# Two transformer blocks on one core: the second tile's norm as a sum of two scaled terms, and four reorderings

## The reference, cut to what matters

```python
def rms_norm(x, g):
    y = x * rsqrt(mean(x * x) + EPS)
    return y * g

h = rms_norm(x, g[0]); m = mixer(h)
x = x + rms_norm(m, g[1])           # post norm, residual
h = rms_norm(x, g[2])               # pre norm of the feed-forward layer
x = x + rms_norm(squared_relu_mlp(h, w1, w2), g[3])

def squared_relu_mlp(h, w1, w2):
    return square(relu(h @ w1)) @ w2
def conformer_conv(h, ...):         # second mixer: three biases are added
    u = h @ w_pw1 + b_pw1           # gate, 31-tap convolution + b_dw, layer norm, silu
    return u @ w_pw2 + b_pw2
```

## Time and profile before

| | |
|---|---|
| median of 3 runs | 923.44 us (922.0 to 924.53) |
| profiled execution, its time | 923.78 us |
| its span | 922.0 us |
| TensorE matmuls busy | 901.8 us, 98% |
| VectorE busy | 689.9 us, 75% |
| POOL, ACT busy | 284.0 us, 268.9 us |
| HBM | 173 GB/s over the span |
| mean granted TensorE clock | 0.997 |

### The profile page before, as it was taken

The page is one execution under the profiler, slowest core; times in us unless marked ns, Lnnn a source line. Parts: engine busy times, 40 slices in busy tenths (PEclk is TensorE's granted clock), DMA queues, the critical chain, the costliest instruction groups (busy, mean ns, idle before and its releaser), DMA issues.

```text
span 922.0 us, 13057 instructions
## 1 busy us (share of the span) xinstructions
PE 901.8 (98%) x4934; PEld 756.7 (82%) x4934; DVE 689.9 (75%) x725; ACT 268.9 (29%) x550; POOL 284.0 (31%) x182
## 2 busy tenths in 40 slices
PE   8999999999999999999999999999999999999997
PEld 6987788888887787688888888888867888888886
DVE  5779879777777775769877777669787687676774
ACT  3537441111112511342111111455586411111112
POOL 5100055444442332136444443200000243333331
PEclk9999999999999999999999999999999999999999
DMA  8851625655558265216655555366502356556641
GB/s 290 283 204 79 219 85 200 226 182 182 182 195 276 99 208 183 92 46 228 201 200 198 200 200 178 107 226 215 219 1 81 104 196 216 190 179 211 192 137 46
DMA packets 82376, 160.29 MB, mean 174 GB/s; under 512 B 5065, under 2 KB 40667, under 8 KB 82337
## 3 DMA queue, kind: packets, MB, share of 16 engines
q1 hardware_dynamic: 82176, 159.68, 50.5%
q10 hardware_dynamic: 160, 0.07, 0.0%
HBM read 158.68 MB, written 1.05 MB: 173 GB/s over the span
## 4 chain that ended last, share of the span: by engine, by line
PE 85%; DVE 8%; ACT 3%; issue 2%; POOL 1%; DMA 1%; DVEq 0%; SPq 0%; POOLq 0%; ACTq 0%
PE ps L1930 82%; PE ps L1934 3%; DVE w_lo L750 2%; ACT arena L1480 1%; DMA x_res<-in_x 1%; ACT w_hi L1476 1%; POOL st L638 0%; ACT arena L1831 0%; DVE nrm L839 0%; DVE st L1292 0%; DVE act_hl L1101 0%; DVE x_res L836 0%; ACT arena L1627 0%; POOL st L637 0%; DVE arena L1416 0%
## 5 line engine op out<-in xcount | busy, mean ns | idle before, releaser
L750 DVE TENSOR_TENSOR w_lo<-raw,w_hi 128x2048 fp32r<-128x2048 f32 (+3 forms) x140 | 325.9, 2354 | 40.0 <-POOL w_hi L731 21.7
L1930 PE MATMUL ps<-act_hl,w_hi 128*128 128x512 f32 (+1 forms) x1088 | 242.0, 369 | 3.6 <-DVE act_hl L909 2.6
L1930 PEld LDWEIGHTS ps<-act_hl,w_hi 128*128 128x128 f32 x1088 | 183.7, 191 | 33.8 <-issue 3.6
L1930 PE MATMUL ps<-w_hi,hl 128*128 128x512 f32 (+2 forms) x680 | 186.7, 384 | 0.6 <-DVE w_lo L750 0.6
L617 POOL TENSOR_SCALAR w_hi<-raw 128x2048 fp32r<-128x2048 f32 x56 | 137.3, 2452 | 157.3 <-PE ps L1930 148.5
L1930 PE MATMUL ps<-w_hi,act_hl 128*128 128x512 f32 (+3 forms) x656 | 181.1, 381 | 2.4 <-DVE w_lo L750 2.4
L1930 PEld LDWEIGHTS ps<-w_hi,hl 128*128 128x128 f32 (+1 forms) x680 | 125.7, 189 | 24.0 <-issue 0.8
L1930 PEld LDWEIGHTS ps<-act_hl,w_lo 128*128 128x128 f32 x1024 | 135.9, 190 | 8.4 <-DVE w_lo L750 0.3
L1930 PEld LDWEIGHTS ps<-w_hi,act_hl 128*128 128x128 f32 x656 | 118.6, 188 | 27.0 <-issue 4.1
L1930 PE MATMUL ps<-act_hl,w_lo 128*128 128x256 f32 (+1 forms) x1024 | 139.4, 281 | 0.0
L1930 PE MATMUL ps<-w_lo,hl 128*128 128x512 f32 (+1 forms) x356 | 108.4, 378 | 0.0
(11 more groups left out here) (212 smaller groups left out, 741.0 us busy)
## 6 DMA issues: line engine op xcount, KB each, us to landing
raw<-in_mlp_w SPq DMA_DIRECT2D x64, 1024.0 KB, 5.2
raw<-in_w_gate SPq DMA_DIRECT2D x22, 512.0 KB, 3.9
raw<-in_w_up SPq DMA_DIRECT2D x22, 512.0 KB, 4.9
raw<-in_w_down SPq DMA_DIRECT2D x11, 1024.0 KB, 5.0
raw<-in_odd_w_pw SPq DMA_DIRECT2D x16, 512.0 KB, 5.4
raw<-in_w_in SPq DMA_DIRECT2D x8, 1024.0 KB, 6.1
raw<-in_even_w_in SPq DMA_DIRECT2D x6, 1024.0 KB, 5.6
raw<-in_even_w_out SPq DMA_DIRECT2D x4, 1024.0 KB, 6.8
```

The source lines that it names most:

```text
L750: tt(w_lo[slot_of(n)][:, 0:w], raw[slot_of(n)][:, 0:w], w_hi[slot_of(n)][:, 0:w].bitcast(F32), ALU.subtract).then_inc(S("w_split"), 1)
L1930: return pe.matmul(o, l, r, start=start, stop=stop, skip_group_check=True)
```

## The change

Seven edits; none changes what is computed beyond rounding.

1. **Second tile at boundaries 1 and 3.** Instead of `x = x + g*r; n = x*p` (g the gained output, r the post scale, p the pre gain), the tile's norm is `n = (g*p)*r + x*p`. `x*p` goes to a scratch tile `pre_1` in one 128x1024 operation behind the first tile's norm; `g` goes to a scratch tile `post_1`; `g*p` is made by halves before r is known; then two operations give `n`, and two more add the residual afterwards.
2. **Opening, ACT and VectorE.** ACT squares tile 0's half, then writes tile 0's high parts, and only then squares both halves of tile 1; VectorE no longer squares tile 1.
3. **Opening, POOL.** The copy of piece 1 goes ahead of rsqrt 1.
4. **First MLP's end.** The last piece is split before `bias_low(0)`.
5. **Second mixer.** The four bias matmuls move into `turn_normed`, ahead of the transpose of tile 1's fifth group.
6. **Third mixer's entry.** The low parts of pieces n and n+1 for tile 1 follow their high parts at once, and free their buffers there.
7. **Third mixer's entry.** Piece n+4's product takes the terms of `w_lo` last, and waits for the split only before them.

```diff
                 def first_rsqrt(m):
-                    gp.wait_ge(S("first_sq"), m + 1)
-                    gp.wait_ge(S("second_sq"), m + 1)
+                    gp.wait_ge(S("first_sq"), 2 * m + 1)
+                    gp.wait_ge(S("second_sq"), 1)
...
                 first_rsqrt(0)
-                hi_until(0)
+                hi_until(1)
                 first_rsqrt(1)
...
+                def gain_half_1(h):
+                    g = norms[0]
+                    dve.wait_ge(S("ssq"), ssqs[0] + h + 1)
+                    link(tt(post_1[:, half[h]], tall_out(ACC, 1)[:, half[h]], gain[g % 4][:, half[h]], ALU.mult))
+                def pre_half_1(h):
+                    link(tt(nrm[:, 1, half[h]], post_1[:, half[h]], gain[(norms[0] + 1) % 4][:, half[h]], ALU.mult))
+                def add_pre_1(g):
+                    next_rstd()
+                    ssqs[0] += 4
+                    for h in half:
+                        stt(nrm[:, 1, h], nrm[:, 1, h], rs_post[:, 1:2], pre_1[:, h], ALU.mult, ALU.add)\
+                            .then_inc(S("normed"), 1)
+                    for h in half:
+                        stt(x[:, 1, h], post_1[:, h], rs_post[:, 1:2], x[:, 1, h], ALU.mult, ALU.add)\
+                            .then_inc(S("x_new"), 1)
...
                     if s in SCALE_LATER:
                         post_add_pre(s, 0, g + 1)
+                        link(tt(pre_1, x[:, 1, :], gain[(g + 1) % 4][:, :], ALU.mult))
+                        gain_half_1(0)
                     else:
                         post_add(0)
                         pre_tile(0, g + 1)
-                    post_gain(1, 0)
+                        post_gain(1, 0)
                     low_tile(0, TURN_BANK[s])
-                    post_gain(1, 1)
                     if s in SCALE_LATER:
-                        post_add_pre(s, 1, g + 1)
+                        pre_half_1(0)
+                        gain_half_1(1)
+                        pre_half_1(1)
+                        add_pre_1(g + 1)
                     else:
+                        post_gain(1, 1)
...
                 first_norm(0)
-                first_square(1)
                 first_low(0)
...
+                    lo_until(n0 + 4 * MLP_BLOCKS - 1)
                     if s == 0:
-                        lo_until(n0 + 4 * MLP_BLOCKS - 2)
                         bias_low(0, bias_pw1)
-                    lo_until(n0 + 4 * MLP_BLOCKS - 1)
...
+                act.wait_ge(S("x_in0"), 16)
+                first_square(0, 0)
+                act.wait_ge(S("gain_col"), 1)
+                first_high(0)
+                act.wait_ge(S("x_in1"), 16)
+                first_square(1, 0)
+                first_square(1, 1)
+                first_high(1)
...
+                            if m == 1 and k == 4:
+                                for b in range(4):
+                                    mm(ps[:, ACC + b, :], sel[:, b % 2, :], bias_pw2, True, False)
...
                         narrow(j, m, False)
+                        if m == 1 and j < 2:
+                            narrow(j, 1, True).then_inc(S("pe_piece"), 1)
                 lows[0] += TILE_LOWS
-                for j in range(4):
-                    if j >= 2:
-                        arrived(n + j)
-                        narrow(j, 0, True)
+                for j in range(2, 4):
+                    arrived(n + j)
+                    narrow(j, 0, True)
                     narrow(j, 1, True).then_inc(S("pe_piece"), 1)
...
-                    tall(n + 4 + q, UP, act_hl, 2 * q, q == 0, q == 3, 2, 1024)
+                    tall(n + 4 + q, UP, act_hl, 2 * q, q == 0, q == 3, 2, 1024, low_last=q == 0)
```

More of the change, by code:

```diff
@@ L302, in two_blocks @@
         gain_rows = AR(2048, P, p=KD)
+        post_1, pre_1 = AR(4608, D), AR(5632, D)
         gain_col = st[:, 176:176 + KD]
@@ L1536, in high_of_turned, with first_square, first_high @@
                         act_high(turned(bank, 2 * j, 2), 2 * j, 2)
[L1539 to L1544, removed]
+                def first_square(m, h):
+                    f(junk[:, m, 512 * h:512 * h + 512], x[:, m, 512 * h:512 * h + 512], ACT.Square, scale=1.0 / D ** 0.5,
+                      accum_out=ssx[:, 2 * m + h:2 * m + h + 1]).then_inc(S("first_sq"), 1)
+                def first_high(m):
                     for k0 in range(0, KD, TILE_STEP[m]):
@@ L2378, in _ @@
                 turn_normed()
-                for m in range(M):
-                    for h in range(2):
-                        mm(ps[:, ACC + 2 * m + h, :], sel[:, h, :], bias_pw2, True, False)
                 tall(FIRST["pw2"], ACC, act_hl, 0, False, False, 2, 1024, k_waits=(lows[0] + 1, lows[0] + 2))
```

## The result

The changed kernel takes 926.72 us (median of 6 runs, 926.22 to 927.63) against 923.43 us before (median of 6, 922.0 to 924.53): a ratio of 1.0042, 95% interval [1.0031, 1.0052]. It is slower by 0.42%, just beyond the 0.3% that was called no change. The time is 0.9 us over the forecast of 925.8 and inside its range, but it lies in the case "slower by over 0.3%" (0.29), not in the likeliest one, "within 0.3%" (0.60). Its profiled execution has a span of 924.7 us.

The account below looks back on a forecast made before the run. It took TensorE's work plus its waits as the bound (PE 85% of the chain). 923.78 + 4.4 (opening) + 0 (boundaries) - 0.95 - 0.3 - 0.8 = 926.1, so 925.8 us as a median; range 920.8 to 928.0.

Parts of the forecast that it names:

- slower by over 0.3%: Whole kernel: the changed kernel takes above 926.2 us; chance 0.29.
- within 0.3%: Whole kernel: a time from 920.7 to 926.2 us, not to be told from no change; chance 0.60.
- The queue in the opening: Opening: both POOL copies get ahead of `lo(0)`, low part starts at 21.4, 3.2 later, less a 0.32 wait: 2.9 lost.
- The clock in the opening: Opening: after idling, TensorE runs at the lower clock again, costing 1.5 us more, bounds 0 and 6.
- the lower clock lasts: Opening, rival: lower clock lasts into tile 1's high parts; at 3.0 us the run is 927.3; chance 0.15.
- nearly 2 us in hand: Opening, before: tile 0's split ended at 16.48, but TensorE came to the low part only at 18.21.
- from an extra of 1.9 on: Opening: if the lasting lower clock costs an extra 1.9 us or more, the run is over 926.2.
- Boundaries 1 and 3: Edit 1: the 0.62 wait goes but returns ahead of the hidden block: 0 each, between -0.6 and +0.5 us.
- before 136.2: Boundary 1: the forecast is wrong if VectorE reaches the hidden block before 136.2 us.
- First MLP's end: Edit 4: TensorE resumes 1.3 us earlier, part is kept: -0.95 us, between -0.3 and -1.6.
- Bias: Edit 5, second mixer: four bias matmuls fall into TensorE's waits of 0.23 and 0.28: -0.3 us, between 0 and -0.5.
- Third mixer: Edits 6 and 7, third mixer's entry: the 0.78 wait goes: -0.8 us, between 0 and -0.8.

Follow-up runs that it names:

- the runs with the fillers: Changed kernel plus 13 filler matmuls, results unread, before, between and behind tile 1's transposes in the opening: 923.52 us, ratio 1.0008.
- run of the split put later: Changed kernel with edits 2 and 3 undone and, in each MLP, VectorE's last split behind the hidden block's first square: 920.16 us, ratio 0.9967.
- the lower group: Three runs, mean clock 0.998 and 0.999, of the changed kernel with edits 2 and 3 undone: 919.4 to 919.6 us.
- the run with the old opening: Changed kernel with edits 2 and 3 undone, all else kept: 920.2 us, ratio 0.9969.
- low parts in the old order: Changed kernel with edits 2, 3 and 7 undone: 921.3 us in a single run.
- copies held back: Changed kernel with one wait added on POOL, so the copy of piece 2 waits until piece 0 is split: 921.63 us, ratio 0.9977.
- norm as before: Changed kernel with edits 1, 2 and 3 undone: 921.55 us, ratio 0.9978.
- the one with the 12 fillers: Changed kernel with edits 2 and 3 undone and 12 instead of 4 filler matmuls ahead of the first high-part product: 919.7 us, ratio 0.9967.

## Why the prediction was right, and where not

The main mechanism was right, but that the point is off by only 0.9 us is partly luck: two errors of opposite sign nearly cancelled. The opening cost 5.66 where the sum had 4.4, and the rest gave back 2.95 where it had 2.05, so the trace of after less that of before gives +2.7 where the sum had +2.35. The other 0.55 comes from going over to the median: the profiled run of before lay 0.34 over its median, that of after 0.21 under (926.51 against 926.72).

- **The queue in the opening: right.** Forecast 2.9, measured 2.68 - 0.32 = 2.4. Alternation with both copies, `lo(0)` last, `rstd` at 14.44 (14.65), all as written; the low part 0.5 early (20.89 for 21.4). That this is the cause is shown: holding the copies back takes norm 1 from 4.16 to 0.89.
- **The clock in the opening: the step that failed.** The prediction said "so I take the same price again", 1.5 us. Measured: 1.49 in the low part (start to start 3.47 for 2.30, and the wait of 0.32 that went) and 1.81 in the high parts (5.82 for 4.01), 3.3 in all; the runs with the fillers give 3.3. The fall of before lasted from about 12.2 to 15.6, this one from 18.3 to 28.6. The price was taken from an episode behind one wait of 2.33 us and put on one in which four waits (0.56, 1.01, 1.39, 1.08) lie within 8 us. The slower rival, "the lower clock lasts", had it at 3.0 and 927.3. It is what happened: 925.8, 1.8 more for the clock, 0.5 less for the queue, 0.9 won elsewhere and the 0.55 above give 926.7. It deserved more than 0.15, as its evidence for (more than twice the stretch) was stronger than its evidence against (the eight transposes in it).
- **What the opening was compared with.** The profiled run of before had itself a fall that not every run has. Without it the opening ends at 23.00 (run of the split put later), so the change costs 7.2 there, not 5.66: 4.2 of start, less 0.32, and 3.3 of clock. The "nearly 2 us in hand" of the forecast were mostly this fall: without it TensorE comes to the low part at 16.71, 0.2 behind the end of the split at 16.48, and the 1.5 of the clock were not hidden but stood in the time of before (24.52 against 23.00). By the lower group that is 919.4 + 7.2 = 926.6. The forecast's "from an extra of 1.9 on" was thus sound only on average over the runs.
- **Boundaries 1 and 3: sign right, size off.** Forecast 0 each, measured -0.29 and -0.32. The wait went and came back ahead of the hidden block as described (0.69, within "0.5 to 0.9"), but took back only 0.4 of the 0.7 gained. VectorE reached the block 0.28 earlier than before (136.22 in the run with the old opening, 136.50 before), since it made part of `pre_1` in what had been idle time; in the trace of after, 141.87 less the 5.66 of the opening is 136.21, at the very edge of the "before 136.2" that was to prove the forecast wrong.
- **First MLP's end: right.** -0.95 forecast, -0.98 measured, wait 0.36 (0.3). **Bias: nearly right.** -0.3, measured -0.28 at the product's start and -0.20 a pair of matmuls later.
- **Third mixer: the cap was wrong.** -0.8 was also its lower bound, since the bracket had 0.78; measured -1.06. At boundary 1 the same holds: 0.69 went where the bracket had 0.62. A bracket is less than what the wait costs, in part because the first matmuls behind a wait take longer (0.73 for a pair, 0.62 for the next pair); this is 0.1 of the 0.28, the rest is not accounted for.
- **Chances.** With the middle at 925.8 and the bound of "slower" at 926.2, 0.60 against 0.29 put too much weight inside the bound; the terms with a hidden upper end (clock 0 to 6) should have moved it.

## What to carry to other kernels

Before starting an engine's work sooner, write down which waiting work of a third engine then falls on the critical one: here a start 1.3 us earlier was bought with a norm 1.65 us later, which let two copies in ahead of a split that TensorE needed, and one wait on the copying engine took 5.1 of the 6.5 us back. Give an idle stretch of TensorE two prices, its length and what the following matmuls cost at the lower clock, and take the second as open upward. When a difference of a few tenths of a per cent is at stake, look at the runs' mean clocks first, and compare runs of the same clock.

## What the runs showed of the hardware that was not expected

- **A fall of the granted clock belongs to a run, not to a kernel.** The old opening's wait had a fall to 0.50 behind it in the profiled runs of before and of two experiments (waits of 2.33, 2.37 and 2.40; the 32 matmuls took 5.53 to 5.57). It had none in that of the low parts in the old order (wait of 1.78, 4.07), and none in the run of the split put later, with a wait of 2.34:

```profile
12.02 4.06 PE L1965 MATMUL ps<-act_hl,w_hi 128*128 128x256 f32 x32 [2.34 <-DVE act_hl L936]
...
16.71 1.98 PE L1965 MATMUL ps<-act_hl,w_lo 128*128 128x128 f32 x16
```

- **There is a second place.** In the third mixer's attention the clock was 0.50 from 676 to 679 us in two profiled runs (copies held back, low parts in the old order), from 677.5 to 681 in a third (norm as before) and in none of the others; TensorE's longest wait in the 15 us ahead of it was 0.39. Just ahead of it TensorE ran 32 small matmuls (64x15, from 673.2 in the run with the low parts in the old order), but it ran them in the traces without a fall too. Such a fall costs about 1.5 us: 5.56 for 4.06 in the opening, and here the run with the low parts in the old order is 0.16 behind the one with the 12 fillers at 620.8 and 1.76 behind it at 684. That is the step between most runs of a kernel: before has 922.0 to 922.6 in some and 923.1 to 924.7 in most of the rest, with a few at 925.1 to 925.6. The mean clock does not sort them fully, though. Of the 25 runs of before recorded at 0.999, 16 lie at 922.0 to 922.6 and 9 at 923.1 to 923.5; what costs those 9 a microsecond no trace shows. Why one run has it and the next not stays open; no run here separates it from the exact time at which the work arrives.
- **The new opening falls in all runs.** All 5 or 6 runs of each of the three kernels with edit 2, no fillers and no wait on POOL have a mean clock of 0.993 to 0.995.
- **Two operations with a waiting copy take the copy in between.** Norm 1's two halves, 0.89 together, took 4.16 and 4.15 beside two copies of 1.9. The engines took turns instruction by instruction. That doing the norm in two halves makes it worse is not shown: no run has the norm in one operation, and where the second copy fell on the split instead (TensorE kept busy) the low part was as late.
